# A two-layer decoder trunk on one core: norm factors applied to projection results, and the first layer's gate units moved ahead of its attention

## The chip, the cores and the metric

One core of a Trainium2 chip runs one launch of the whole step. The metric is device time in microseconds (us) of that launch. The median of three runs of the kernel before is 1759.73 us (1757.77 to 1759.96).

## What is computed

The tokens are 512 of a prompt and 64 of eight samples (8 each), 576 columns in all, with a model width of 1024. Two layers follow each other:

```
for layer in (0, 1):
    h = rms_norm(x, g_mix[layer])
    # layer 0: forgetting attention (8 heads of 64) || spatial gating of width 512
    # layer 1: stick-breaking attention            || short gated convolution of width 512
    x = x + concat(attention(h), side(h)) @ w_out
    h = rms_norm(x, g_mlp[layer])
    x = x + square(relu(h @ w_up)) @ w_down        # 1024 -> 4096 -> 1024
y = rms_norm(x, g_final)

rms_norm(x, g) = x * rsqrt(mean(x*x) + 1e-6) * g    # one factor per token, one gain per channel
```

The samples attend to 1024 past positions each, gathered page by page (128 rows) from caches in HBM: 64 pages of keys and 64 of values per layer, 256 KB each. Besides y, the new keys, values, log forget gates, normalised gate rows and convolution tails are outputs.

Two facts matter below. The factor of a token (call it r) is the same for all channels, so it can be multiplied in before a projection or into its result. And the gain g depends on the channel, so it has to be in the input.

## The kernel before, in words

**Layout.** Activations lie with channels on the 128 partitions and the 576 tokens along the free dimension: X (the residual stream) is 8 chunks of 128x576. Products are taken in a split form: every operand is cut into a high part and a low rest (HH and HL for activations, WH and WL for weights), and a product is the sum of high x high, low x high and high x low.

**Units.** All projections are done in units. A unit is one 128-column block of weights (WR, 128x1024, 512 KB) against all 576 tokens: 8 chunks x 3 products x 2 halves of 288 tokens = 48 matmuls into a pair of PSUM banks (`unit`, L1395; the body loop of `unit_loop`, L209). There are 188 units: 4 + 12 + 4 in the first layer's input projection (4 gate columns "g", 12 for q, k and v, 4 for the side branch), 8 for its output, 64 for its MLP, and 24 + 8 + 64 in the second layer. ScalarE cuts the high part of the weights two units ahead (`cut_high`, `next_high`, L531 to L547), VectorE takes the rest (`cut_low`, L846), and SyncE loads the raw block once the rest is cut (`load_weights`, L362). There are two sets of weight buffers and two pairs of banks for units. Semaphores count: `unit_done` (TensorE), `evac_act` and `evac_dve` (a result has left PSUM), `w_high`, `w_low`. A unit starts when its weights are cut and both engines have emptied the unit two before it.

**Norm** (`norm`, L583 and L890; `rms`, L1418; `pair_after_norm`, L1415). After the last unit of a stage, ScalarE squares the chunk, VectorE adds it to SQS, TensorE multiplies SQS by ones to sum over channels, VectorE and ScalarE turn that into R (the factor r, laid out on all partitions), and then for each of 8 chunks VectorE multiplies X by gain and R into TMP, ScalarE cuts HH, VectorE takes HL. The first two units of the next stage are interleaved chunk by chunk (`first_pair`), so that they can follow the chunks.

**Attention** (20 slots, `for k in range(SLOTS)`, L1683 on TensorE, L761 on ScalarE, L1295 on VectorE). A slot handles one of 16 prompt tasks (a pair of heads and a block of 128 queries) in four steps spread over slots, four key pages (`page`: 4 turns of 128x128 into PSUM bank BK, then one copy to KTB by ScalarE or VectorE) and a share of the samples' work. The side branch's units are cut in halves (`half_unit`, L1663, 24 matmuls into bank BU) and laid between: the first layer's 8 halves one each in slots 0 to 7, the second layer's 24 in slots 0 to 17. The next page's turns wait until the last page has been copied, since both use BK:

```
if n >= 1:
    name, count = page_copied(L, n - 1)
    pe.wait_ge(S[name], count)
```

**Queues.** SyncE issues all large loads in program order and waits in that order. GpSimd issues 64 small loads of the cached log gates (`lf_raw`, L478), the constants of the gating branch and the stores. The first layer's order on TensorE is: turn x, norm 0, the four g units, wait for all `lf_raw`, forget logits, turn g, twelve q/k/v units with the gating products between them, turn k and v to rows, attention.

**End.** After the last unit: norm 4 writes Y, TensorE turns Y, VectorE copies it to XN (L1375), and GpSimd issues two stores (L520, L521).

## Time and profile before

| | us |
|---|---|
| median of three runs | 1759.73 |
| the profiled execution | 1760.2 |
| its span in the trace | 1758.2 |
| TensorE matmul busy | 1560.7 (89%) |
| TensorE weight load busy | 1446.0 (82%) |
| VectorE busy | 737.9 (42%) |
| ScalarE busy | 527.2 (30%) |
| GpSimd busy | 54.0 (3%) |

The span is what the trace covers from the first instruction to the last; the execution's own time has about 2 us around it. Matmuls are pipelined, so a busy TensorE says that matmuls were in flight, not that the array is at its peak: what a unit costs is read from how long a run of units takes. Busy shares are averages over stages with different limits, and so the views by stage count more than this table. The granted TensorE clock averages 0.942 of full speed over the span.

### The profile page before, as it was taken

How to read it: one execution, taken by the hardware profiler on the slowest of the kernel's cores; microseconds unless marked ns; L12 is line 12 of the kernel's file. 1: busy time of each engine (PE TensorE's matmuls, PEld its weight loads, DVE VectorE, ACT ScalarE, POOL GpSimd, SP SyncE). 2: the span in 40 equal slices, each digit the busy share in tenths (PEclk: the TensorE clock that was granted, in tenths of full speed). 3: DMA queues.
4: the chain of work that ended last, by engine and by line, in shares of the span. 5: the costliest groups of instructions: out<-in, count | busy, mean ns of one | idle time of the engine just before them, and what ended most of it. 6: DMA issues, size and time to landing. Idle time of an engine off the chain costs nothing.

```text
span 1758.2 us, 31539 instructions
## 1 busy us (share of the span) xinstructions
PE 1560.7 (89%) x12022; PEld 1446.0 (82%) x12022; DVE 737.9 (42%) x1142; ACT 527.2 (30%) x860; POOL 54.0 (3%) x124
## 2 busy tenths in 40 slices
PE   4599988777889999999989998887789999999994
PEld 3599865446889999999989886665689999999994
DVE  5244444432444434343352355556354433434334
ACT  3121233321233313132232245556133322313120
POOL 4410000000000000000000000000000000000000
PEclk9799899887989999999989999999889999999997
DMA  4123356642212223323242345664222222222221
GB/s 141 40 80 86 121 150 198 189 142 84 84 48 84 84 76 87 87 73 94 73 132 84 108 141 155 194 181 138 65 72 60 84 85 83 85 83 84 84 72 54
DMA packets 239074, 178.65 MB, mean 102 GB/s; under 512 B 9860, under 2 KB 203464, under 8 KB 238986
## 3 DMA queue, kind: packets, MB, share of 16 engines
q1 hardware_dynamic: 234282, 168.62, 33.2%
q0 software_dynamic: 4704, 8.88, 1.5%
q8 instruction: 53, 0.87, 0.2%
q14 instruction: 35, 0.29, 0.1%
HBM read 170.20 MB, written 7.26 MB: 101 GB/s over the span
## 4 chain that ended last, share of the span: by engine, by line
PE 81%; DVE 5%; ACT 5%; issue 4%; DMA 2%; POOLq 1%; POOL 1%; SPq 1%; DVEq 0%; ACTq 0%
PE BP L1395 58%; PE BU L1673 4%; PE BP L1410 4%; PE BK L1547 4%; PE BD L1656 2%; PE BD L1628 2%; PE BP L1585 1%; POOLq L477 1%; PE BK L1608 1%; PE BP L1598 1%; ACT WH L537 1%; ACT KTB L654 1%; PE BD L1635 1%; DVE WL L848 1%; POOL lf_raw L478 1%
## 5 line engine op out<-in xcount | busy, mean ns | idle before, releaser
L1395 PE MATMUL BP<-HH,WH 128*128 128x288 f32 x1536 | 332.8, 299 | 18.4 <-DVE ffL L886 7.9
L1395 PE MATMUL BP<-HL,WH 128*128 128x288 f32 x1536 | 331.2, 298 | 0.0
L1395 PE MATMUL BP<-HH,WL 128*128 128x288 f32 x1536 | 331.0, 298 | 0.0
L848 DVE TENSOR_TENSOR WL<-WR,WH 128x1024 fp32r<-128x1024 f32 x188 | 230.1, 1224 | 105.2 <-ACT WH L537 73.1
L1395 PEld LDWEIGHTS BP<-HH,WH 128*128 128x128 f32 x1536 | 250.4, 191 | 19.7 <-ACT TMP L576 8.3
L1395 PEld LDWEIGHTS BP<-HL,WH 128*128 128x128 f32 x1536 | 250.4, 191 | 0.0
L1395 PEld LDWEIGHTS BP<-HH,WL 128*128 128x128 f32 x1536 | 250.0, 191 | 0.0
L547 ACT ACTIVATE WH<-WR 128x1024 fp32r<-128x1024 f32 x159 | 167.2, 1051 | 240.8 <-PE BP L1395 240.4
L1395 PE MATMUL BP<-ffH,WH 128*128 128x288 f32 x1024 | 218.9, 295 | 0.0
L1395 PE MATMUL BP<-ffL,WH 128*128 128x288 f32 x1024 | 218.3, 294 | 0.0
L1395 PE MATMUL BP<-ffH,WL 128*128 128x288 f32 x1024 | 216.9, 293 | 0.0
L872 DVE TENSOR_TENSOR X<-BP,X 128x288 f32 (+1 forms) x160 | 65.8, 453 | 263.8 <-PE BP L1395 263.8
L1395 PEld LDWEIGHTS BP<-ffL,WH 128*128 128x128 f32 x1024 | 163.7, 188 | 0.0
L1395 PEld LDWEIGHTS BP<-ffH,WL 128*128 128x128 f32 x1024 | 163.7, 187 | 0.0
L1395 PEld LDWEIGHTS BP<-ffH,WH 128*128 128x128 f32 x1024 | 162.9, 187 | 0.0
L884 DVE TENSOR_TENSOR TMP<-TMP 128x576 f32<-128x576 f32 x64 | 48.5, 758 | 168.8 <-ACT TMP L576 168.8
L1547 PEld LDWEIGHTS BK<-ident,KR 128*128 128x128 f32 x512 | 61.2, 150 | 65.1 <-issue 59.4
L1547 PE MATMUL BK<-ident,KR 128*128 128x128 f32 x512 | 87.4, 297 | 27.1 <-ACT KTB L654 16.9
L576 ACT ACTIVATE TMP<-BP 128x288 f32<-128x288 f32 x128 | 45.5, 408 | 199.6 <-PE BP L1395 199.6
L654 ACT ACTIVATE KTB<-BK 128x512 f32<-128x512 f32 x80 | 47.7, 596 | 148.5 <-PE BK L1547 143.6
L1138 DVE COPY KTB<-BK 128x512 f32<-128x512 f32 x48 | 33.2, 691 | 124.8 <-PE BK L1547 121.8
L1673 PE MATMUL BU<-HH,WH 128*128 128x288 f32 x256 | 79.4, 310 | 0.0
(296 smaller groups left out, 1738.1 us busy)
## 6 DMA issues: line engine op xcount, KB each, us to landing
WR<-in_w_up_dram SPq DMA_DIRECT2D x64, 512.0 KB, 4.1
WR<-in_w_down_dram SPq DMA_DIRECT2D x64, 512.0 KB, 3.9
KR<-in_cache_fox_k_dram SPq DMA_DIRECT2D x64, 256.0 KB, 2.8
VR<-in_cache_fox_v_dram SPq DMA_DIRECT2D x64, 256.0 KB, 3.0
VR<-in_cache_sb_v_dram SPq DMA_DIRECT2D x64, 256.0 KB, 3.2
KR<-in_cache_sb_k_dram SPq DMA_DIRECT2D x64, 256.0 KB, 2.8
WR<-in_w_in_odd_dram SPq DMA_DIRECT2D x24, 512.0 KB, 4.1
WR<-in_w_in_even_dram SPq DMA_DIRECT2D x20, 512.0 KB, 4.0
```

The source lines that it names most:

```text
L547: A(WH[1 - u][:], WR[1 - u][:], ACT.Copy).then_inc(S["w_high"], 1)
L576: last = A(TMP[:, u, h * TH:(h + 1) * TH], B[2 * u + h][:, 0:TH], ACT.Relu)
L654: A(KTB[:, n // 4 % 2, :, n % 4 * P:(n % 4 + 1) * P], BK[:, :].rearrange("p (c k) -> p c k", c=CT), ACT.Copy).then_inc(S["kt_act"], 1)
L848: V.tensor_tensor(WL[u][:], WR[u][:], WH[u][:].bitcast(F32), ALU.subtract).then_inc(S["w_low"], 1)
L872: last = V.tensor_tensor(x, B[2 * u + h][:, 0:TH], x, ALU.add)
L884: V.tensor_tensor(TMP[:, u, :], TMP[:, u, :], TMP[:, u, :], ALU.mult).then_inc(S["relu_squared"], 1)
L1395: last = M(B[2 * u + h][:, 0:TH], w[u][:, k, :], x[:, k, h * TH:(h + 1) * TH], start=(k == 0 and n == 0), stop=(k == KT - 1 and n == 2))
L1410: last = M(B[2 * u + h][:, 0:TH], w[u][:, k, :], x[:, k, h * TH:(h + 1) * TH], start=(m == 0 and n == 0), stop=(m == KT - 1 and n == 2))
L1547: last = TR(BK[:, c * P:(c + 1) * P], KR[:, n % 4, c * P:(c + 1) * P], ident[:])
L1628: last = M(BD[32 * c:32 * c + 32, o * 512:(o + 1) * 512], QB[:, c, p, s:s + 2, :], KTB[:, grp % 2, c, :], start=(L == 1 and s == 0), stop= ...
L1656: last = M(B5[32 * c:32 * c + 32, 0:P], PTS[:, 4 * (g % 2) + jj, c, s:s + 2, :], v_tile(g, jj)[:, c * P:(c + 1) * P], start=False, stop=(g ...
L1673: last = M(BU[:, 0:TH], w[u][:, k, :], x[:, k, h * TH:(h + 1) * TH], start=(k == 0 and n == 0), stop=(k == KT - 1 and n == 2))
```

## The change

It has these parts.

1. **The factor r leaves the input.** The high and low parts of an activation chunk are now cut from X times gain alone (`lift` on ScalarE, `lift_low` on VectorE), right after that chunk's residual unit has been added (`evac_lift`). r (tile R, or R1 for the second layer's input projection) is multiplied in as VectorE empties a unit's banks (`evac_in`, `evac_up`), since VectorE now empties both halves. `evac_act` is gone. The first unit of a stage waits chunk by chunk for `norm_low`, and the sum of squares and its matmuls come behind that unit.
2. **A third weight set** for unit 2 of each output projection and of the first stage, with banks 4 and 5; its cutting waits for no unit.
3. **The start.** x is loaded in two column halves with the first two weight blocks between them; turns of x and chunks of the first pair alternate; the constants of the gating branch are loaded early by SyncE.
4. **The first layer's order.** Forget logits and the cached log gates come after ten of the twelve q/k/v units. The four side units are whole units before the attention, with the turns of k and v among them. Turns of g, k and v use two banks. No half units are left in the first layer's attention.
5. **First layer's attention.** Key pages alternate between banks BK and BU (`page_bank`); the samples' `sample_top` and `sample_exp` come one slot earlier.
6. **The second layer's side branch** takes three multiplications of a 128x576 tile by R1 for each of four blocks, on GpSimd, and VectorE's `conv_in` and `gate_half` wait for them (`side_scaled`).
7. **The MLP** reads its input from new tiles H2H and H2L; HH and HL serve as one of the two buffers of the hidden layer. relu and r are one VectorE operation out of PSUM; the square moves to ScalarE.
8. **The end.** Y is X times gain; its turns lie between the last units (`turn_y`), r is found per row with a small matmul, and rows are scaled and stored one block of 128 rows after the other by SyncE.

Of the diff, its core, in the order of the file: planning, then SyncE, GpSimd, ScalarE, VectorE and TensorE.

```diff
+        def page_bank(L, n):
+            return B[6 + n % 2] if L == 0 else B[6]
...
-        SIDE_OUT = [{9: (0, 1), 10: (2, 3)}, {18: (0, 1, 2, 3)}]
+        SIDE_OUT = [{1: (0, 1), 2: (2, 3)}, {18: (0, 1, 2, 3)}]
...
+            load_x(0)
...
+            load_first(0)
+            load_first(1)
+            load_x(1)
+            load_first(2)
...
                 if L == 1:
+                    for c in range(CT):
+                        for step2 in range(3):
...
+                            g.tensor_tensor(RES[:, c, :], RES[:, c, :], R1[:], ALU.mult).then_inc(S["side_scaled"], 1)
...
+            def lift(z):
+
+                dst = {1: H2H, 2: HH, 3: H2H, 4: Y}[z]
                 def body(g, i, u, more):
                     next_high(g, u, more)
...
+                    act.wait_ge(S["evac_dve"], g + 3)
+                    gain = vec[:, NORM_G[z] + i:NORM_G[z] + i + 1]
+                    if z < 4 or i < KT - 1:
+                        A(dst[:, i, :], X[:, i, :], ACT.Copy, scale=gain).then_inc(S["norm_high"], 1)
+                    A(TMP[:, u, :], X[:, i, :], ACT.Square).then_inc(S["squared"], 1)
...
-                        last = A(TMP[:, u, h * TH:(h + 1) * TH], B[2 * u + h][:, 0:TH], ACT.Relu)
-                    last.then_inc(S["evac_act"], 1)
...
+                    act.wait_ge(S["up_relu"], i + (m0 + 1))
+                    A(TMP[:, u, :], TMP[:, u, :], ACT.Square).then_inc(S["relu_squared"], 1)
...
+            def evac_in(tile_of, r, scale=None):
...
                     for h in range(2):
...
+                        if scale is None:
+                            last = V.tensor_tensor(t, z, s, ALU.mult)
+                        else:
+                            last = V.scalar_tensor_tensor(t, z, scale, s, ALU.mult, ALU.mult)
                     last.then_inc(S["evac_dve"], 1)
...
+            def lift_low(z, k, dst, src):
+
+                gain = vec[:, NORM_G[z] + k:NORM_G[z] + k + 1]
+                dve.wait_ge(S["norm_high"], z * KT + k + 1)
+                V.scalar_tensor_tensor(dst[1][:, k, :], X[:, k, :], gain, dst[0][:, k, :].bitcast(F32), ALU.mult, ALU.subtract
+                                       ).then_inc(S["norm_low"], 1)
...
+                    for h in range(2):
+                        s = slice(h * TH, (h + 1) * TH)
+                        last = V.scalar_tensor_tensor(TMP[:, u, s], B[2 * u + h][:, 0:TH], 0.0, R[:, s], ALU.max, ALU.mult)
+                    last.then_inc(S["up_relu"], 1)
                     dve.wait_ge(S["ff_high"], i + (m0 + 1))
...
+            def unit(hi, lo, z=None):
+                def body(g, i, u, more=None, mid=None, wset=None, bank=None):
                     pe.wait_ge(S["w_low"], g + 3)
-                    pe.wait_ge(S["evac_act"], g + 1)
-                    pe.wait_ge(S["evac_dve"], g + 1)
...
                     for k in range(KT):
+                        if z is not None:
+                            pe.wait_ge(S["norm_low"], z * KT + k + 1)
...
+                    unit_loop(pe, unit(HH, HL), q + 8, 2)
+                    past_rows()
+                    forget_logits()
+                    unit_loop(pe, unit(HH, HL), q + 10, 2)
+                    forget_turn()
+                    past_tail()
+                    pe.wait_ge(S["evac_dve"], q + 12 + 2)
+                    natural(NG, 2 * NG, 2)
+                    unit_loop(pe, unit(HH, HL), G_SIDE[0], 2)
+                    forget_sums()
+                    natural(2 * NG, 3 * NG, 2)
+                    unit_loop(pe, unit(HH, HL), G_SIDE[0] + 2, 2)
...
-                    if n >= 1:
-                        name, count = page_copied(L, n - 1)
+                    back = 2 if L == 0 else 1
+                    if n >= back:
+                        name, count = page_copied(L, n - back)
                         pe.wait_ge(S[name], count)
...
+                        if n == 0:
+                            first = 2
+                            unit(H2H, H2L, 1 + 2 * L)(g, 0, 0)
+                            rms(1 + 2 * L)
+                            unit(H2H, H2L)(g + 1, 1, 1)
```

Three places show the new order. The first is TensorE at the start of the program, before the change; XN holds x as rows, BP are the banks of the units.

```order
L1434 MATMUL BP<-ident,XN 128x128 x4
L1435 MATMUL BP<-ident,XN 128x64
L1421 MATMUL BP<-SQS,ones 128x288 x2
L1410 MATMUL BP<-HH,WH_55 128x288 x2
L1410 MATMUL BP<-HL,WH_55 128x288 x2
L1410 MATMUL BP<-HH,WL_57 128x288 x2
```

And after it:

```order
L1587 MATMUL BD<-ident_62,XN_91 128x128 x4
L1588 MATMUL BD<-ident_62,XN_91 128x64
L1556 MATMUL BP0<-HH_50,WH0_55 128x288 x2
L1556 MATMUL BP0<-HL_51,WH0_55 128x288 x2
L1556 MATMUL BP0<-HH_50,WL0_57 128x288 x2
L1556 MATMUL BP1<-HH_50,WH1_56 128x288 x2
L1556 MATMUL BP1<-HL_51,WH1_56 128x288 x2
L1556 MATMUL BP1<-HH_50,WL1_58 128x288 x2
L1587 MATMUL BK<-ident_62,XN_91 128x128 x4
```

The sum of squares no longer stands between the turns of x and the first unit; a turn and a chunk of the first pair alternate.

The second is VectorE between the last unit of the first output projection and the first units of the MLP, before the change; WL_57 and WL_58 are the two low weight sets.

```order
L876 TENSOR_TENSOR SQS<-SQS,TMP 128x576
L220 REGISTER_ALU
L220 COMPARE_AND_BRANCH
L848 TENSOR_TENSOR WL_58<-WR_54,WH_56 128x1024
L894 TENSOR_SCALAR R<-BP 128x288 x2
L896 MEMSET SQS 128x576
L902 SCALAR_TENSOR_TENSOR TMP<-X,vec,R 128x576 x2
L911 TENSOR_TENSOR HL<-TMP,HH 128x576
```

And after it:

```order
L949 TENSOR_TENSOR X<-BP,X 128x288 x2
L960 SCALAR_TENSOR_TENSOR H2L<-X,vec,H2H 128x576
L965 TENSOR_TENSOR SQS<-SQS,TMP 128x576
L922 TENSOR_TENSOR WL_58<-WR_54,WH_56 128x1024
L1005 TENSOR_SCALAR R<-BD 128x288 x2
L1007 MEMSET SQS 128x576
L993 SCALAR_TENSOR_TENSOR TMP<-BP,R 128x288 x2
L996 TENSOR_TENSOR HL<-TMP,HH 128x576
L922 TENSOR_TENSOR WL_57<-WR_53,WH_55 128x1024
```

The chunk's low part (H2L) is cut before R exists; R now stands ahead of the first result's way out of PSUM, and the next weight block (WL_57) behind it.

The third is TensorE in slots 1 and 2 of the first layer's attention, before the change; L1547 are turns of a key page, L1673 a half unit, L1628 the samples' scores.

```order
L1547 MATMUL BK<-ident_62,KR_92 128x128 x12
L1585 MATMUL BP0<-PA_90 128x128 x2
L1589 MATMUL BP0<-FR_110,twin_71 128x128 x2
L1591 MATMUL BP0<-neg_causal_r_69,ident_r_64 128x128 x2
L1626 MATMUL BD<-DR_109,PICK_128 128x512
L1628 MATMUL BD<-KTB_104,QB_127 32x512 x4
L1547 MATMUL BK<-ident_62,KR_92 128x128 x4
L1673 MATMUL BU<-HH_50,WH1_56 128x288
L1673 MATMUL BU<-HL_51,WH1_56 128x288
L1673 MATMUL BU<-HH_50,WL1_58 128x288
```

And after it:

```order
L1722 MATMUL BK<-ident_62,KR_94 128x128 x4
L1722 MATMUL BU<-ident_62,KR_94 128x128 x4
L1760 MATMUL BP0<-PA_92 128x128 x2
L1764 MATMUL BP0<-FR_115,twin_71 128x128 x2
L1766 MATMUL BP0<-neg_causal_r_69,ident_r_64 128x128 x2
L1801 MATMUL BD<-DR_114,PICK_136 128x512
L1803 MATMUL BD<-KTB_109,QB_135 32x512 x4
L1722 MATMUL BK<-ident_62,KR_94 128x128 x4
L1722 MATMUL BU<-ident_62,KR_94 128x128 x4
L1803 MATMUL BD<-KTB_109,QB_135 32x512 x4
```

The half unit has gone from between the pages, and the pages alternate between two banks.

## Rows read from the trace of the kernel before

**Rows 1.** The page: TensorE's busy time, and its granted clock in 40 slices.
```profile
PE 1560.7 (89%) x12022; PEld 1446.0 (82%) x12022; DVE 737.9 (42%) x1142; ACT 527.2 (30%) x860; POOL 54.0 (3%) x124
...
PEclk9799899887989999999989999999889999999997
```

**Rows 2.** Stretches: length, busy us by engine (instructions), granted clock, DMA share, GB/s.
```profile
101.67:197.20 95.53, 95.53 (x731) 93.00 (x729) 40.91 (x76) 19.74 (x31) 6.53 (x13) 1.00 0.28 76
197.20:291.30 94.10, 79.64 (x691) 61.63 (x689) 39.77 (x96) 25.64 (x58) 2.32 (x4) 0.91 0.59 180
291.30:381.30 90.00, 70.10 (x627) 43.83 (x626) 36.99 (x80) 29.52 (x74) 0.00 (x0) 0.87 0.62 182
381.30:416.66 35.36, 20.96 (x214) 12.77 (x213) 12.28 (x26) 9.05 (x21) 0.00 (x0) 0.74 0.43 126
416.66:475.60 58.94, 55.53 (x384) 55.07 (x384) 20.10 (x29) 11.55 (x14) 0.00 (x0) 0.93 0.23 66
475.60:503.84 28.24, 16.90 (x100) 16.16 (x101) 18.86 (x27) 11.40 (x18) 0.00 (x0) 0.82 0.13 36
503.84:899.40 395.56, 395.53 (x2976) 395.29 (x2976) 153.54 (x193) 109.02 (x160) 0.00 (x0) 1.00 0.29 82
899.40:925.61 26.21, 17.01 (x105) 16.25 (x105) 17.81 (x26) 11.07 (x16) 0.52 (x1) 0.80 0.56 162
992.00:1242.82 250.82, 209.04 (x1901) 163.30 (x1901) 134.49 (x220) 129.87 (x219) 4.23 (x7) 0.92 0.54 159
1301.70:1329.91 28.21, 16.85 (x101) 16.11 (x101) 18.87 (x27) 11.41 (x18) 0.00 (x0) 0.82 0.13 36
1725.50:1758.20 32.70, 9.83 (x44) 7.24 (x44) 15.61 (x30) 2.05 (x3) 1.30 (x2) 0.61 0.20 72
```

**Rows 3.** TensorE in order of time, the start: us, length, idle before it and its releaser.
```profile
11.86 1.11 PE L1434 MATMUL BP<-ident,XN 128*128 128x128 f32 x4
...
38.23 0.82 PE L1410 MATMUL BP<-HH,WH 128*128 128x288 f32 x2 [4.88 <-DVE HL L911]
...
86.78 0.48 PE L1460 MATMUL BU<-ident,lf_raw 64*128 64x64 f32 x2 [16.73 <-DMA lf_raw<-in_cache_fox_logf_dram]
```

**Rows 4.** TensorE's waits in the first layer's attention (197 to 416 us): total, times, longest.
```profile
PE BK L1547 <- ACT KTB L654: 13.8, 16, 2.1
PE BD L1635 <- ACT SN L731: 10.1, 4, 3.9
```

**Rows 5.** The half units alone (L1673), first eight slots and next eight: us, busy, clock.
```profile
197.20:291.30 94.10, 27.99 (x192) 26.34 (x192) 0.91 0.59 180
```

**Rows 6.** Two page turns, in order of time, and a stretch of slots without half units.
```profile
338.40 0.65 PE L1547 MATMUL BK<-ident,KR 128*128 128x128 f32 x4
...
362.15 1.12 PE L1547 MATMUL BK<-ident,KR 128*128 128x128 f32 x4
...
319.50:350.20 30.70, 23.59 (x234) 14.56 (x234) 15.87 (x34) 13.16 (x35) 0.00 (x0) 1.00 0.71 206
```

**Rows 7.** TensorE at unit 2 of the first output projection, in order of time.
```profile
435.34 0.70 PE L1395 MATMUL BP<-HH,WH 128*128 128x288 f32 x2 [3.31 <-ACT TMP L563]
```

**Rows 8.** Groups of instructions: busy us, mean ns of one | idle before, releaser.
```profile
L848 DVE TENSOR_TENSOR WL<-WR,WH 128x1024 fp32r<-128x1024 f32 x188 | 230.1, 1224 | 105.2 <-ACT WH L537 73.1 <-ACT WH L547 24.9
L547 ACT ACTIVATE WH<-WR 128x1024 fp32r<-128x1024 f32 x159 | 167.2, 1051 | 240.8 <-PE BP L1395 240.4 <-issue 0.2
L872 DVE TENSOR_TENSOR X<-BP,X 128x288 f32 x148 | 60.9, 453 | 257.4 <-PE BP L1395 257.4
L884 DVE TENSOR_TENSOR TMP<-TMP 128x576 f32<-128x576 f32 x64 | 48.5, 758 | 168.8 <-ACT TMP L576 168.8
L579 ACT ACTIVATE ffH<-TMP 128x576 f32 x60 | 41.1, 686 | 55.4 <-DVE TMP L884 55.4
L460 POOL TENSOR_SCALAR_AFFINE_SELECT upto<-upto 128x128 f32<-128x128 f32 x1 | 0.3, 282 | 0.0
```

801 lines of the change are left out of this document (465 added, 336 removed).

## The prediction, made before the changed kernel had run

> **What bounds the kernel now.** I read the page first, then the trace by stretches, then the waits inside the stretches where TensorE stands still. In the page TensorE's matmuls are in flight for 89% of the span and the granted clock is at its upper level (2.4 GHz, a 9 in the row of slices) except near the stage ends and in the attentions [rows 1]. The stretches say what kind of bound that is. In the first MLP 62 units take 395.56 us, 6.38 us each or 0.133 us per matmul, with TensorE busy all the time at clock 1.00 [rows 2]: there only fewer matmuls would help, and the change removes none. But each stage end is a hole: 28.24, 26.21 and 28.21 us for one norm and a first pair, in which 96 of the 100 to 105 matmuls are the pair's, at a clock of 0.80 to 0.82 [rows 2]. The last 32.70 us hold 44 matmuls [rows 2]. In the first layer's attention TensorE is busy 79.64 of 94.10 and 70.10 of 90.00 us [rows 2]. So what this change can gain lies in the holes, and I price each hole by what of it has to stay. The sum stands against the profiled execution of 1760.2 us, 0.5 above the median of the three runs; I subtract from the median.
>
> **1. Start to attention (0 to 197.2 us).** Gone from the path: the sum of squares and the factor before the first unit (which started at 38.23 [rows 3]) and the 16.73 us for the 64 small gate loads [rows 3], now waited for ten units later. The first pair may start once half of x and two weight blocks are there and cut: turns began at 11.86 [rows 3], and a cut is 1.05 + 1.22 us [rows 8], so between 12 and 16, and I take 13. Then 96 matmuls x 0.133 = 12.8, six turns laid between (4 + 1 instructions, 0.85 us at full clock from 0.65 [rows 6]) = 5.1, and 3.5 more since the early part will run at the lower clock (a turn took 1.11 us [rows 3]): 34.4. Two more gate units (12.8) and the moved sum of squares (0.9) end at 48.1, or about 48.7 with hand-offs, where they ended at 70.05 (86.78 less its idle time, [rows 3]): -21.3. The loads' wait goes with about 2 us of lower clock behind it: -18.7. The four side units come in: 4 x 6.38 = +25.5. SyncE gets eleven small loads of gating constants ahead of unit 3's block, which TensorE wants some 28 us later than the first: free. Against that stand new joints: k and v are turned in two banks instead of four, so that each turn waits for the copy two before it, forget logits and log-gate rows stand between units with VectorE's new evacuations ahead of them, and the attention begins behind an evacuation and not behind a turn. No row shows them; bounds are 2 us (all covered) and 22 us (every one of 15 turns waits 0.8 and a few long waits); I take 12, since such a single-bank wait costs about 0.86 us each (13.8 in 16 [rows 4]). Together **-2.5**, ends -12 and +8.
>
> **2. First layer's attention (197.20 to 416.66, 219.5 us).** Eight half units leave: 27.99 us of matmuls [rows 5]. What that is worth is open. The slots with halves took 94.10 us, the next eight without 90.00 [rows 2]: a difference of 4.1, the lower bound; 28.0 is the upper. Slots 8 to 15 do more of the samples' work and ran at 0.87 instead of 0.91, so 4.1 is too little; and a half covered copies and transfers. I take -18. The waits for a key page's copy, 13.8 us in 16 [rows 4], are what two banks remove, with some 2.5 us of shorter ones: -16.3. `sample_exp` one slot earlier answers the four waits for SN, 10.1 us [rows 4]; I leave 2: -8. The first output weights are now loaded and cut inside the attention, where the rest of the block (1.22 us [rows 8]) and its hand-offs used to hold the first output pair: -3.2. Sum -45.5, taken as **-46**, ends -26 and -75. What comes next as a bound is the transfers: 128 pages of 256 KB are 33.6 MB, and at the 206 GB/s seen without halves [rows 6] that is 163 us, just under the 173.5 that I forecast; the far end would need 232 GB/s.
>
> The clock is the doubt here. A page turn took 0.65 us at the upper level and 1.12 at the lower (1.2 GHz) [rows 6]; but 319.50:350.20, a stretch without any half unit, had clock 1.00 throughout, with 234 matmuls busy 23.59 of 30.70 us [rows 6]. From that row I count no further loss. The Trainium skill, "TensorE: Matmul & The Clock Gate", Part 4, says that transposes in PE mode don't count as activity for the full clock; by that rule, taking the half units from between the turns would leave the array idle in the clock's eyes. The trace disagrees for the stretch named, since it is mostly turns and scores; by the rule term 2 would be about +27 instead of -46, and the total 1730 (rival A).
>
> **3. Output projections.** Unit 2 waited 3.31 us for banks and weights [rows 7], and so did the second layer's; the third set and banks 4 and 5 remove both, and about 1.2 us of lower clock behind each: **-9**, ends -6 and -11.
>
> **4. The three norm transitions.** The pair's 96 matmuls at 0.133 are 12.8 us, and the sum's two matmuls about 1.24; the rest of 28.24, 26.21 and 28.21 [rows 2] is 14.2, 12.2 and 14.2. It goes if the first unit of the next stage follows the last residual unit. It can: after each residual unit VectorE does two additions of 453 ns, one low cut (about 0.76) and a sum of squares (0.76), a weight rest (1.22), together 3.7 us; ScalarE copy, square and high cut, about 2.5 us [rows 8]; both below 6.38. Only the last chunk is late: 0.9 + 0.69 + 0.76 is 2.4 us behind its unit, while the first unit's seven earlier chunks last 5.6 us. What comes late next is R: first needed when unit 0 leaves PSUM, it is ready about 2.4 us after the sum; with two relu operations, square, copy and a low cut (0.9 + 0.69 + 0.69 + 0.76, and 1.22 for a weight rest in between) the chain is about 7.2 us against unit 1's 6.38. So about 1 us comes back twice, at each MLP's start: -40.6 + 2.6 = **-38**, ends -30 and -42.
>
> **5. The end.** Of the 32.70 us [rows 2], the norm, turns and copies after the last unit shrink to: last addition 0.9, last chunk's Y and square 1.4, sum and factor about 3, scaling and store of a block of 512 KB. I keep 19.9. The turns of Y now lie between units: 7 x 0.75 = +5.3 on a busy TensorE. **-7.5**, ends -12 and -4.
>
> **6. Second layer's attention (250.82 us).** TensorE is busy 209.04 of it, VectorE 134.49 [rows 2]. GpSimd gets 12 multiplications of 128x576. The one near row is 282 ns for 128x128 [rows 8]; by elements that is 1.27 us each, 15.2 in all, on an engine with 4.23 us of work in this stretch [rows 2]. The side branch's results are needed only at the last slot. **0**, ends 0 and +15 (all of it held against VectorE, or the last block late). If the cover by half units were gone, each of the four blocks would cost its 3.8 us.
>
> **7. The MLP units.** VectorE takes over ScalarE's relu out of PSUM and ScalarE the square. Per up unit VectorE: 2 x 0.45, 0.76 and 1.22 = 2.9 us; ScalarE: 0.69 + 0.69 + 1.05 = 2.4 us; both below 6.38. 0, end +2.
>
> Sum: -2.5 - 46 - 9 - 38 - 7.5 = -103. **1759.7 - 103 = 1657 us.**
>
> **Rivals.**
> A, the clock falls in the first layer's attention. With no long units between the pages the stretch stays at the lower level. For it: the clock is 0.74 in 381.30:416.66, where the least work is dense [rows 2]; page turns then cost 1.12 for 0.65 [rows 6]. Against it: the row of 1.00 without halves [rows 6]. Price: TensorE's work there is 79.64 + 70.10 + 20.96 - 27.99 = 143 us [rows 2, 5]; times 1.12 / 0.65 it is 246, with no wait left, where I forecast 173: +73, 1730. A partial fall, +20 to +40, is likelier than the full one.
> B, GpSimd holds VectorE. The twelve multiplications stand in the side branch's chain and run beside VectorE's work on the same tiles. Price +15: 1672. The Trainium skill, "GPSIMD Engine Reference", sections 3.1 and 4.1, gives an elementwise operation of two inputs on GpSimd about twice VectorE's time (4497 against 2293 ns for 2048 elements) and says that the two share SBUF ports; an estimate from that is 1.26 us for 576 elements. No row of this kernel shows the sharing.
> C, the transitions don't close. If the first unit still waits for the stage's end (its low chunk held by the weight rest ahead of it on VectorE, or the sum of squares ahead of the cut), term 4 is about -5: 1690. Against it: in the order of the changed kernel the low cut stands directly behind the additions.
> D, slower than before, in the up-projections. The chain from a unit's end to the next use of its buffers is now two VectorE operations, square, copy, low cut and the two weight cuts on the same engines: 0.9 + 0.69 + 0.69 + 0.76 + 1.05 + 1.22 = 5.3 us with everything in a row. It decides once it exceeds 6.38; it would have to be 8.0 us (2.7 us of hand-offs) for 64 up units to lose 103 us and end above 1760. For it: VectorE now does what two engines did at every unit's exit, and TensorE's next unit waits on that alone. Against: busy sums of 2.9 and 2.4 us.
>
> **How the numbers follow.** The forecast, with its terms inside their ends, has 0.72; A in full 0.04, in part 0.09; B 0.07; C 0.05; D 0.03, mostly past the point where it ends above 1760. The independent ends added as squares give about -20 and +35 around 1657, so the forecast's own range is 1637 to 1692; a part of A, and a gain beyond my ends in the attention, are to be held too: **1630 to 1700**. Outside lie A in full, most of D and a little on either side of the forecast, together under 0.2. A measurement here tells about 0.2%, 3.5 us, from no change; only D and a full A with B and C reach it: faster 0.96, same 0.01, slower 0.03.
>
> **What would show it.** In the changed profile: the first matmul of the first pair (L1556) at 13 us and q units from 48; the attention from about 195, with key turns alternating BK and BU and few waits for KTB, no wait of 3.9 us for SN, ending near 368 at a mean clock of at least 0.87; no idle time over 4 us on TensorE at the three stage ends, but about 1 us at the MLPs' third unit; up and down units at 6.38 us; the second attention within 2 us of 250.8; a tail near 20 us. It is wrong if the granted clock of the first attention is under 0.75 (A), if TensorE waits for `side` work or conv steps in the second (B), if the first unit's idle time names norm_low of an early chunk (C), or if units of the MLP take more than 6.5 us (D).

## The result, and the profile after

The changed kernel takes 1626.75 us (median of 4, 1626.14 to 1632.39); the kernel before, run beside it, 1758.75 (1756.65 to 1759.96). The ratio is 0.9258 with a 95% interval of 0.9235 to 0.9281: faster by 132 us, where 103 were forecast. The time lies 3 us below the stated range of 1630 to 1700.

The page of the changed kernel, the rows that answer to [rows 1]:

```profile
PE 1520.4 (94%) x12030; PEld 1412.5 (87%) x12030; DVE 730.4 (45%) x1200; ACT 518.5 (32%) x776; POOL 65.2 (4%) x123
...
PEclk9999999989999999999999999898899999999998
```

TensorE runs 12030 matmuls where it ran 12022: the work is nearly the same, and what has gone is time in which it stood or ran slowly. The mean granted clock went from 0.942 to 0.970.

The stretches that answer to [rows 2]: start; first attention; first output projection; transition to the MLP; the other 62 units of the first MLP; second norm and input projection; second attention; output projection; transition; second MLP with the turns of Y; the tail. Columns as there.

```profile
0.00:191.23 191.23, 173.02 (x1244) 164.23 (x1245) 95.59 (x197) 43.08 (x55) 41.19 (x102) 0.99 0.41 112
191.23:355.37 164.14, 134.61 (x1332) 85.67 (x1333) 74.69 (x158) 57.30 (x147) 0.52 (x1) 0.90 0.66 196
355.37:407.70 52.33, 52.33 (x386) 52.33 (x387) 26.59 (x40) 16.55 (x22) 0.00 (x0) 0.98 0.22 64
407.70:421.43 13.73, 13.73 (x101) 13.29 (x99) 7.25 (x12) 6.00 (x8) 0.00 (x0) 1.00 0.25 73
421.43:815.30 393.87, 393.29 (x2979) 393.29 (x2979) 161.27 (x232) 113.66 (x138) 0.00 (x0) 1.00 0.29 86
815.30:894.36 79.06, 78.14 (x586) 77.50 (x584) 28.41 (x45) 15.39 (x16) 0.51 (x1) 1.00 0.36 104
894.36:1146.64 252.28, 209.81 (x1900) 161.53 (x1901) 138.04 (x221) 130.81 (x220) 22.95 (x19) 0.91 0.53 158
1146.64:1199.20 52.56, 52.56 (x385) 52.56 (x386) 24.96 (x36) 15.16 (x20) 0.00 (x0) 0.97 0.25 72
1199.20:1213.01 13.81, 13.81 (x102) 13.36 (x100) 7.25 (x12) 6.00 (x8) 0.00 (x0) 1.00 0.25 73
1213.01:1610.20 397.19, 396.61 (x3008) 396.61 (x3009) 158.87 (x234) 112.60 (x137) 0.00 (x0) 1.00 0.27 80
1610.20:1624.50 14.30, 2.49 (x20) 2.13 (x18) 7.53 (x16) 1.94 (x6) 0.00 (x0) 0.63 0.44 165
```

Read it as a ledger. The transitions are now pure matmul time: 13.73 us busy of 13.73, where [rows 2] shows 16.90 of 28.24. The second norm with the input projection, which after the change is the stretch 815.30:894.36, was before it

```profile
899.40:992.00 92.60, 82.76 (x585) 81.79 (x586) 34.92 (x48) 24.13 (x35) 0.52 (x1) 0.93 0.36 103
```

so that the whole ledger, forecast beside measured, is this (profiled executions; each measured number is the difference of unrounded lengths above and in [rows 2]; before the change the second output projection was 1242.82:1301.70 and the second transition with its MLP 1301.70:1725.50):

| stage | before | after | measured | forecast |
|---|---|---|---|---|
| start | 197.2 | 191.2 | -6.0 | -2.5 |
| first attention | 219.5 | 164.1 | -55.3 | -46 |
| output projections | 58.9 + 58.9 | 52.3 + 52.6 | -12.9 | -9 |
| three transitions with what follows | 423.8 + 92.6 + 423.8 | 407.6 + 79.1 + 407.7 | -45.9 | -38 |
| second attention | 250.8 | 252.3 | +1.5 | 0 |
| tail, with Y's turns between units | 32.7 | 14.3 + 3.3 | -15.1 | -7.5 |
| sum | 1758.2 | 1624.5 | -133.7 | -103 |

(The 3.3 is 397.19 less 393.87: seven turns of Y, 0.47 us each; it is taken out of the second MLP's 411.0 and put to the tail.) The signs are right (for the second attention nothing was forecast), and every gain was put too low: the miss of 30 us is spread over the stages, with 9.3 in the first attention, 7.9 in the transitions, 7.6 in the tail, 3.9 in the output projections and 3.5 in the start.

What TensorE still waits for between 190 and 400 us (total, times, longest):

```profile
PE BD L1818 <- ACT PTS L815: 6.5, 4, 1.6
PE BD L1831 <- DMA VR<-in_cache_fox_v_dram: 6.4, 5, 3.1
PE BD L1827 <- DVE PTN L1400: 5.3, 4, 1.6
...
PE BK L1722 <- ACT KTB L717: 1.2, 2, 0.8
```

KTB's 13.8 us in 16 waits [rows 4] are down to 1.2 in 2, and SN's 10.1 in 4 to 0.3 in 1. The waits for the samples' next steps and for the value pages' transfers grew a little: PTS was 3.5 before the change, PTN 4.0, VR 5.1.

### The profile page after: what moved, and what is told of

Its sections match the earlier page's. It is cut to its first block, busy times and chain, and to the rows that moved or that the text cites. A ratio compares the mean times of both kernels' runs of the same rounds, so it can differ in the third digit from the quotient of the medians.

```text
span 1624.5 us, 30903 instructions
## 1 busy us (share of the span) xinstructions
PE 1520.4 (94%) x12030; PEld 1412.5 (87%) x12030; DVE 730.4 (45%) x1200; ACT 518.5 (32%) x776; POOL 65.2 (4%) x123
## 4 chain that ended last, share of the span: by engine, by line
PE 85%; DVE 5%; ACT 4%; issue 2%; SPq 2%; DMA 2%; POOL 0%; DVEq 0%; ACTq 0%
PE BP L1547 64%; PE BU L1848 3%; PE BP L1556 3%; PE BK L1722 2%; PE BD L1831 2%; PE BD L1803 2%; PE BD L1547 1%; PE BP L1760 1%; SPq L436 1%; DMA VR<-in_cache_fox_v_dram 1%; ACT PP L724 1%; SPq L437 1%; PE BP L1773 1%; ACT KTB L717 1%; PE BD L1638 0%
## 5 line engine op out<-in xcount | busy, mean ns | idle before, releaser
L1547 PE MATMUL BP<-HH,WH 128*128 128x288 f32 x1120 | 239.8, 296 | 0.5 <-DVE WL L922 0.5
L1547 PE MATMUL BP<-HH,WL 128*128 128x288 f32 x1120 | 238.8, 295 | 0.0
L1547 PE MATMUL BP<-HL,WH 128*128 128x288 f32 x1120 | 238.7, 295 | 0.0
L1547 PE MATMUL BP<-H2H,WH 128*128 128x288 f32 x1024 | 218.8, 295 | 1.2 <-DVE WL L922 1.2
L1547 PE MATMUL BP<-H2L,WH 128*128 128x288 f32 x1024 | 218.8, 294 | 0.0
L1547 PE MATMUL BP<-H2H,WL 128*128 128x288 f32 x1024 | 217.2, 293 | 0.0
L1547 PEld LDWEIGHTS BP<-HH,WH 128*128 128x128 f32 x1120 | 179.7, 188 | 1.1 <-DVE WL L922 0.7
L1547 PEld LDWEIGHTS BP<-HH,WL 128*128 128x128 f32 x1120 | 179.8, 188 | 0.0
L1547 PEld LDWEIGHTS BP<-HL,WH 128*128 128x128 f32 x1120 | 179.8, 188 | 0.0
L1547 PEld LDWEIGHTS BP<-H2H,WH 128*128 128x128 f32 x1024 | 163.2, 187 | 1.8 <-issue 1.6
L1547 PEld LDWEIGHTS BP<-H2H,WL 128*128 128x128 f32 x1024 | 163.8, 188 | 0.0
L1547 PEld LDWEIGHTS BP<-H2L,WH 128*128 128x128 f32 x1024 | 163.4, 188 | 0.0
L1547 PE MATMUL BP<-ffL,WH 128*128 128x288 f32 x512 | 109.5, 294 | 0.0
L1547 PE MATMUL BP<-ffH,WH 128*128 128x288 f32 x512 | 109.4, 295 | 0.0
L1547 PE MATMUL BP<-ffH,WL 128*128 128x288 f32 x512 | 108.7, 293 | 0.0
L993 DVE SCALAR_TENSOR_TENSOR TMP<-BP,R 128x288 f32<-128x288 f32 x128 | 52.6, 452 | 118.6 <-PE BP L1547 116.9
```

Of the source, the lines that this page charges most:

```text
L993: last = V.scalar_tensor_tensor(TMP[:, u, s], B[2 * u + h][:, 0:TH], 0.0, R[:, s], ALU.max, ALU.mult)
L1547: last = M(B[b + h][:, 0:TH], w[w0][:, k, :], x[:, k, h * TH:(h + 1) * TH], start=(k == 0 and n == 0), stop=(k == KT - 1 and n == 2))
```

## The experiments

A word on noise first. The first layer's attention, from the first key-page turn to the first output pair, is the same code in eleven of the kernels profiled here (the changed one among them), and took 164.1 to 169.7 us in them, mean 166; the second layer's, from its first key-page turn, 244 to 253.5 in all. So a difference of totals of 5 us, or of 9 where single profiles are compared, says little, and I read an edit's effect in its own stretch of the trace. Differences of the first attention are given against the changed kernel's 164.1; against the mean they are 2 us smaller.

### The first layer's attention

**One bank for key pages.** In the changed kernel:

```diff
-            return B[6 + n % 2] if L == 0 else B[6]
+            return B[6]
...
-                    back = 2 if L == 0 else 1
+                    back = 1
```

> The changed kernel with one bank for the first layer's key pages again. My theory, by the prediction's term 2: the second bank is worth the 13.8 us of KTB waits and 2.5 us of shorter ones, so this kernel takes 14 to 18 us more than 1626.75. Rival: since the half units are gone and the pages now follow each other directly, a single bank would show a wait on nearly every one of 64 pages; at 0.8 us each that is up to 50 us. Second rival: the attention is bound by its loads, and one bank costs under 5 us.

Measured 1660.17 us (+33), and the attention took 193.4 instead of 164.1: +29.3. The waits and the first slots:

```profile
PE BK L1722 <- ACT KTB L717: 21.8, 23, 2.0
```
```profile
192.50:275.00 82.50, 65.58 (x492) 41.66 (x493) 29.68 (x59) 23.79 (x58) 0.52 (x1) 0.73 0.44 128
```

With 2.5 us more for VectorE's copies the waits for KTB come to 24.3, against 2.1 in the changed kernel: 22 us more, of which other waits give back some 4. The other part of the 29 is clock: it is 0.73 here, while the changed kernel's first stretch of this attention shows 0.95 (below), and the same 1332 matmuls are in flight for 146.45 us instead of 134.61, 11.8 more. The forecast of 16.3 was off by the factor 1.8.

**Short half units.** In the kernel before, each first-layer half unit has 2 matmuls instead of 24:

```diff
-                    for k in range(KT):
+                    ks = (0, KT - 1) if L == 0 else range(KT)
+                    for k in ks:
                         for n, (w, x) in enumerate(((WH, HH), (WH, HL), (WL, HH))):
+                            if L == 0 and n != (0 if k == 0 else 2):
+                                continue
```

> The kernel before, with each of the first layer's eight half units cut from 24 matmuls to 2 (the side branch's gate results are left out, their handling stays). It takes off 25.7 of the 28.0 us of matmuls and nothing else. By the prediction's term 2 the path gains 18: 1741 against 1759. Rival one: page copies and clock eat it, gain 4 or less. Rival two (clock, rival A of the prediction): with the long stretches of matmuls gone the granted clock of 197 to 291 us falls clearly under 0.91 and the kernel gains nothing or loses. Rival three: the whole 25.7 shows.

Measured 1747.93 (ratio 0.9923, 0.9901 to 0.9945), 10.6 us less than before; the attention took 211.5 instead of 219.5. So 25.7 us of matmuls were worth 8 (one profile of each kernel; like stretches of the changed kernel differ by up to 5.6). Why, its first slots show:

```profile
198.80:290.00 91.20, 68.50 (x534) 44.17 (x531) 40.94 (x98) 25.82 (x59) 2.26 (x4) 0.79 0.63 195
```
```profile
PE BK L1547 <- ACT KTB L654: 13.7, 13, 5.9
```

The clock fell from 0.91 [rows 2] to 0.79, and in this stretch the KTB waits rose to 13.7 us from this, in the kernel before:

```profile
PE BK L1547 <- ACT KTB L654: 6.0, 6, 2.1
```

This is rival A's mechanism, in part: half units had filled the waits and held the clock up.

**Filler with one bank** tests that the other way round. The kernel with one bank gets work of the half units' size in slots 0 to 7:

```diff
+                    if L == 0 and k < 2 * CT:
+                        pe.wait_ge(S["w_low"], G_OUT[0] + 4)
+                        for n in range(27):
+                            j2 = 2 * (n % 4)
+                            M(BU[:, 0:2 * P], (WH[0] if n % 2 else WL[0])[:, n % KT, :], WH[1][:, j2:j2 + 2, :].rearrange("p k n -> p (k n)"),
+                              start=(n == 0), stop=(n == 26))
```

> The changed kernel with one bank for key pages, and in each of the first layer's slots 0 to 7, where a half unit stood before the change, 27 matmuls of 256 columns on weights that lie there (results not used): about 25 us of TensorE work. The kernel with one bank takes 193.4 us in the attention. If such work covers the waits for page copies and holds the clock up, as the 8.0 us for 25.7 us of matmuls in the kernel with short half units suggests, the attention takes about 202. Rival: work and waits add, and it takes 218.

Measured 202.6 us in the attention, 1666.83 in all. Some 25 us of extra work (216 matmuls, in flight 29.31 us) cost 9.2. The first slots:

```profile
190.70:285.00 94.30, 82.24 (x744) 62.91 (x748) 32.44 (x65) 25.74 (x64) 0.52 (x1) 0.95 0.45 130
```

The clock is 0.95 where it was 0.73, and the KTB waits are 14.2 us where they were 21.8. The covering is seen from both sides: taking such work out gives 8, putting it in costs 9.

**Samples' exp a slot later**, as before the change:

```diff
+                        if p >= 0 and o == 1:
+                            sample_top(p)
...
-                        if p >= 0 and o == 0:
-                            sample_top(p)
```

(and the same for `sample_exp`).

> The changed kernel with the samples' sample_top and sample_exp of the first layer back one slot later, where they were before. By term 2: four waits of TensorE for SN of 2.0 to 2.5 us come back, +8, and perhaps more by lower clock behind them. Rival: the weights are needed no sooner than the second half of their slot, and under 2 us come back.

Measured 1641.48 (+15); the attention 175.2, +11.1, with TensorE's waits for SN at 13.0 us in 4 where the changed kernel has 0.3. As forecast in kind, 3 more in size.

**Late cut of the second output block:**

```diff
-                    cut_high(G_OUT[0] + 1)
...
-                if L == 1:
-                    cut_high(G_OUT[1] + 1)
+                cut_high(G_OUT[L] + 1)
```

(and `cut_low` likewise).

> The changed kernel with the cut of the second output weight block at the end of the first layer's attention again. By term 2 the wait before the first output pair comes back: +3.2; the second layer, where this wait is still there, shows 4.55 us, so +4.5 in the attention's stretch, up to +6 with lower clock. Rival: the pair starts behind the last values' transfers anyway: under 1.

```profile
PE BP L1552 <- DVE WL L920: 3.2, 1, 3.2
```

Measured 1634.04 (+7). The wait is back with the 3.2 us that term 2 had for it; the attention took 170.0, which is hardly outside the noise.

**Those three undone together.**

> The changed kernel with three parts of the first layer's attention undone together: one bank for key pages, sample_top and sample_exp a slot later, and the cut of the second output weight block at the attention's end. If the parts add up as measured alone (29.3 and 11.1 us in the attention's stretch) and the cut is worth 3.3 to 4.5, the stretch takes 164.1 + 29.3 + 11.1 + 4 = 208, close to the 211.5 of the kernel before with short half units. Rival: the parts overlap (waits of one cover those of the other, the clock falls only once), and it takes under 200.

Measured 209.3 us in the attention (sum forecast 208), 1669.39 in all. The parts add up, and what is left to the 211.5 us of the kernel before with short half units is 2.2. Its clock over the whole attention, against that of one bank and of the filler:

```profile
192.20:401.50 209.30, 155.86 (x1332) 96.63 (x1332) 76.22 (x163) 60.85 (x149) 0.52 (x1) 0.80 0.51 152
```
```profile
192.50:385.90 193.40, 146.45 (x1332) 92.23 (x1333) 74.24 (x158) 58.71 (x147) 0.52 (x1) 0.85 0.56 166
```
```profile
190.70:393.30 202.60, 162.54 (x1548) 114.08 (x1549) 74.26 (x158) 58.95 (x147) 0.52 (x1) 0.92 0.55 160
```

The same 1332 matmuls are busy for 134.61 us at clock 0.90 in the changed kernel, 146.45 at 0.85 and 155.86 at 0.80: a hole costs its own length and then the slower matmuls near it.

### The transitions and output projections

**All chunks first.** The first unit waits for all eight low chunks:

```diff
-                            pe.wait_ge(S["norm_low"], z * KT + k + 1)
+                            pe.wait_ge(S["norm_low"], z * KT + KT)
```

> The changed kernel, but the first unit of each of the three stages waits for all eight low chunks before its first matmul instead of for each in turn. The last chunk is ready about 2.4 us after its residual unit: +2.4 x 3 = 7, and up to 1.7 us of lower clock behind each hole: +7 to +12. Rival: since all but the last chunk are ready long before, and the clock doesn't fall for so short a hole: +6 or less.

Measured 1641.96 (+15); in the trace three waits like this one (the last addition, high cut and low cut of term 4, 2.4 there):

```profile
PE BP L1547 <- DVE H2L L960: 2.7, 1, 2.7
```

That is 8.0 us of idle time, and behind one of the three the clock fell as well (1.7 us); from the first output pair on, without the second attention, the kernel is 10.1 us longer. The rest of the 15 lies in the start (1.8), the first attention (0.6) and the second (250.5 against 247.9, 2.6), which is noise.

**Sum first.** The sum of squares' matmuls ahead of the first unit:

```diff
-                            unit(H2H, H2L, 1 + 2 * L)(g, 0, 0)
                             rms(1 + 2 * L)
+                            unit(H2H, H2L, 1 + 2 * L)(g, 0, 0)
```

> The changed kernel with the sum of squares' matmuls ahead of the first unit in the three norm transitions, so that TensorE stands until the last chunk has been squared and added. By my theory only this order and the chunkwise start close the transitions: last addition 0.9, low cut 0.8, square 0.7, addition 0.8 gives 3 to 4 us of idle each and up to 1.7 us of lower clock behind it: +9 to +15 in all, R is then ready earlier, which gives back 0.6 twice. Rival: the transitions close because r has left the input, and the place of the sum matters little: under 5 us.

Measured 1643.52 (+17); three waits of this kind:

```profile
PE BD L1572 <- DVE SQS L965: 3.2, 1, 3.2
```

By the same reckoning this kernel is 11.7 us longer: 9.7 of idle time, and a dip of the clock behind two of the three holes (0.67 and 0.63 in the next 4 us), none behind the first (1.00).

Neither order brings back the 14 us of each old transition. The other 11 us of each I put to what stood before the first matmul only because r was in the input (mean, root, the multiplication by r, the cuts behind it); no run puts r back there, so this cause is argued and not shown.

**Two weight sets.** Unit 2 of both output projections on the ordinary set and banks:

```diff
-            return 2 if g == 2 else 3 if g - 2 in (G_OUT0, G_OUT1) else 0
+            return 2 if g == 2 else 0
```

(and its loads, cuts and banks as for any unit).

> The changed kernel with unit 2 of both output projections on the ordinary weight set and banks again. By term 3 the waits of 3.3 us come back, and 1.2 to 1.7 us of lower clock behind each: +9. Rival: the first pair's two evacuations are now short and early, so only the cuts (1.05 + 1.22) stand after it: +2.3 x 2, under 6.

Measured 1640.69 (1633.86 to 1644.03); in the output stretches two waits of 2.7 us, and the stretches from the first pair to the next sum of squares grew from 58.6 and 58.9 to 61.4 and 63.7: +7.6. The second grew more since the clock was at 0.57 for 3.94 us behind its hole, and at 1.00 behind the first. Between the two readings (6 and 9).

### The MLP units: where VectorE would decide

In each up unit VectorE's relu is done three times (the extra results go into tiles that are overwritten later), and in a second kernel the extra ones in pieces of 72 columns:

```diff
+                    for again in (ffL, ffH):
+                        for n in range(2):
+                            s = slice(n * 288, (n + 1) * 288)
+                            V.scalar_tensor_tensor(again[grp % 2][:, ds(i, 1), s].rearrange("p o t -> p (o t)"), B[2 * u + n // 1][:, n % 1 * 288:(n % 1 + 1) * 288], 0.0, R[:, s], ALU.max, ALU.mult)
```

> The changed kernel with VectorE's relu out of PSUM done three times over in each of 64 up units (two extra results overwritten later): +1.8 us of VectorE per unit, in the chain in front of the square. By the prediction's rival D the chain of 5.3 us would become 7.1 against 6.34 for a unit: +0.76 x 64 = +49. By the other reading VectorE has 2.9 + 1.8 = 4.7 us of work per unit, the chain has two units to end in, and nothing changes: within 2 us.

> As the kernel with the relu done three times, but the two extra results in 16 pieces of 128x72, which should add about 3.6 us of VectorE per up unit: 6.5 us of work against 6.34 for a unit. By the chain reading (rival D) +2.5 x 64 = +160. By the reading that VectorE's sum of work decides, +0.2 x 64 = +13 (0 to +40, as the pieces' duration is not known).

Measured 1641.67 (+15) and 1671.03 (+44); 13.7 and 41.3 us of it in the two MLPs. The chain is seen on VectorE in the changed kernel, one up unit and the next (start, length):

```profile
435.01 0.82 DVE L993 SCALAR_TENSOR_TENSOR TMP<-BP,R 128x288 f32<-128x288 f32 x2 [1.77 <-PE BP L1547]
437.52 0.76 DVE L996 TENSOR_TENSOR HL<-TMP,HH 128x576 f32 x1 [1.69 <-ACT HH L637]
438.39 1.22 DVE L922 TENSOR_TENSOR WL<-WR,WH 128x1024 fp32r<-128x1024 f32 x1
441.36 0.82 DVE L993 SCALAR_TENSOR_TENSOR TMP<-BP,R 128x288 f32<-128x288 f32 x2 [1.74 <-PE BP L1547]
```

and in the kernel with pieces:

```profile
435.08 1.21 DVE L994 SCALAR_TENSOR_TENSOR HL<-BP,R 128x72 f32 x8 [0.29 <-PE BP L1551]
436.21 1.20 DVE L994 SCALAR_TENSOR_TENSOR HH<-BP,R 128x72 f32 x8
437.33 0.81 DVE L997 SCALAR_TENSOR_TENSOR TMP<-BP,R 128x288 f32<-128x288 f32 x2
439.72 0.76 DVE L1000 TENSOR_TENSOR HL<-TMP,HH 128x576 f32 x1 [1.57 <-ACT HH L637]
440.67 1.23 DVE L922 TENSOR_TENSOR WL<-WR,WH 128x1024 fp32r<-128x1024 f32 x1 [0.19 <-ACT WH L603]
```
```profile
PE BP L1551 <- DVE WL L922: 21.3, 46, 2.8
```

A unit's low weights are ready 4.6 us after the unit ahead ended (435.01 to 439.61) in the changed kernel, and 6.8 us (435.08 to 441.90) in the one with pieces; a unit lasts 6.34. So 0.5 us per up unit is over, and 44 / 64 = 0.69 was measured. With three whole relus it is just at the edge (4.6 + 1.8 = 6.4): almost no hole in the matmuls, but the weight loads between units begin to wait (PEld busy 49.26 of 50 us in 430 to 480 us, 50.00 in the changed kernel), and the wait at the MLP's start grows from 0.6 to 2.0. The pieces added 2.2 us and not the 3.6 I expected, and the chain was 4.6 and not 5.3, so the +49 and +160 that I had by rival D's chain were far too much. **The chain reading is still the right one**: VectorE is busy only 36.24 of the 50 us from 430 to 480 in the kernel with pieces, and its own work in such a unit is 5.2 us (1.21 + 1.20 + 0.81 + 0.76 + 1.23), under 6.34, so that the sum of work would have cost nothing. But in the changed kernel the chain has 1.7 us of room, so rival D lost on its number.

### GpSimd in the second attention

The twelve multiplications cut to two columns each:

```diff
-                            g.tensor_tensor(RES[:, c, :], RES[:, c, :], R1[:], ALU.mult)
+                            g.tensor_tensor(RES[:, c, 0:2], RES[:, c, 0:2], R1[:, 0:2], ALU.mult)
```

> The changed kernel with GpSimd's twelve multiplications of the second layer's side branch cut to two columns each (the factor is left out of the rest). By term 6 they are hidden: within 2 us. By rival B they hold VectorE or the side branch: 5 to 15 us less.

Measured 1629.83 (1627.28 to 1632.30), no less than the changed kernel; the second attention took 246.9 us against 247.9. Rival B's 5 to 15 us aren't there. In the changed kernel the group is

```profile
L569 POOL TENSOR_TENSOR RES<-RES,R 128x576 f32<-128x576 f32 x12 | 18.7, 1558 | 169.1 <-ACT RES L770 93.1 <-DVE RES L1353 75.6
```

1558 ns each, longer than the 1.27 us of term 6, and hidden.

### The start and the end

**Both halves of x first**, ahead of the first two weight blocks.

> The changed kernel with both halves of x loaded ahead of the first two weight blocks. The second half is 1 MB and a part; in the changed kernel x's first half was turned from 8.6 us and the pair began at 16.5, held by the cut of the weights. With the second half ahead, the weights land about 4 us later, and so does the pair: +4. Rival: the copies and cuts of chunks bound the start, not the landing: within 1 us.

Measured 1633.30 (+6.6), of which 4.0 in the start; the second attention, at 253.5 the longest of all, makes up the rest. The first matmul of the pair, in the changed kernel and then here:

```profile
16.48 0.82 PE L1556 MATMUL BP<-HH,WH 128*128 128x288 f32 x2 [3.77 <-DVE WL L922]
```
```profile
20.03 0.82 PE L1556 MATMUL BP<-HH,WH 128*128 128x288 f32 x2 [3.77 <-DVE WL L922]
```

3.6 us later, as expected.

**The gates' wait early**, after four units:

```diff
+                    pe.wait_ge(S["lfp_in"], 16 * NB * PG)
                     unit_loop(pe, unit(HH, HL), q, 2)
```

> The changed kernel in which TensorE waits for the 64 small loads of the cached gates after four units, as before the change, without anything else moved. They landed at 86.8 us in the kernel before; the four units now end at 48.8. If they land as late as before, TensorE stands 38 us: +38 and 2 of lower clock. If they land earlier now, since the queues are laid otherwise, the difference is the landing less 48.8.

```profile
PE BP L1547 <- DMA lf_raw<-in_cache_fox_logf_dram: 34.9, 1, 34.9
```

Measured 1663.62 (+37): the loads land at 84 us now, hardly earlier than before. Had the wait stayed in its place, the four units' gain of 21 us would have come down to 3 (83.8 against 86.8); where it stands now, TensorE finds them landed.

**Turns of Y last.** All eight turns and copies behind the last unit.

> The changed kernel with all eight turns of Y and their copies after the last unit, as before the change, but r still found per row and the stores still by block. The measured tail fell by 18.5 us and 7 turns of 0.5 us came between units. If the turns' place is what the tail gained by, this kernel takes about 7 copies x 0.9 + the turns at the lower clock, less 3.5, so +4 to +8. Rival: the tail is short because the norm is a row factor and the stores go out by block; then it is within 3 us.

**Stores last.** All stores of y after the last scaling.

> The changed kernel with the stores of y issued only after the last block has been scaled, instead of each block after its own scaling. Four scalings of 0.7 us are what the first store gains: +2.5 to +4, all of it in the tail of 14.4 us. Rival: the last block's store ends the kernel either way, since the stores before it run beside the scalings: within 1 us.

Measured 1635.94 and 1633.87. Their tails, 20.3 and 16.8 us against 14.3:

```profile
1614.90:1635.20 20.30, 7.67 (x50) 6.19 (x48) 11.86 (x26) 1.94 (x6) 0.00 (x0) 0.70 0.32 117
```
```profile
1614.80:1631.60 16.80, 2.35 (x21) 2.00 (x19) 7.53 (x16) 1.94 (x6) 0.00 (x0) 0.65 0.38 140
```

Turns between units buy 6.0 and cost 3.3 on TensorE: 2.7 net. Storing by block buys 2.5. (The totals rose by more, 9.2 and 7.1; both kernels' first attentions, the same code, were 5.6 and 3.1 us longer.) Of the 18.4 us by which the tail fell, 8.5 are these two if they add, and the other 9.9 I put to r as a factor of a row: in the trace before, mean and root of 576 columns and the multiplications for Y stand ahead of the turns, and now they don't. No run separates that part, so it is argued and not shown.

### A version that beats both

Two waits left in the changed kernel are at the attentions' ends: the last value pages (up to 3.1 and 4.1 us), and 4.6 us for the second output block of the second layer. Of the edits that go at them, the core:

```diff
+                    if s == NGRP + 1:
+                        sp.wait_ge(S["k_turned"], NB * PG * (L + 1))
+                        for jj in range(4):
+                            q = v_page(L, NPAIR - 1, 3, jj)
+                            v = sp.value_load(pages[0:1, q:q + 1], min_val=0, max_val=POOL - 1)
+                            sp.dma_start(KR[:, jj, :], cache_v[L][0][ds(v, 1)].rearrange("o p h d -> (o p) (h d)")
+                                         ).then_inc(S[f"k_in{L}_{jj}"], 16)
...
+                        if k == NTASK + 2:
+                            cut_high(G_OUT[1] + 1)
```

> The first of these two edits alone. My theory: the waits for the last value pages go, 4 to 9 us less than the changed kernel. Rival: the loads are only moved against others, within 2 us.

> The changed kernel with two further edits: the last four value pages of each layer go to the key pages' buffers, free by then, and are loaded two slots earlier; and the second output block of the second layer is cut in slot 18 instead of behind the attention. The waits in question are 1.6 + 3.1 us in the first layer, 1.2 + 4.1 in the second, and 4.55 at the second pair: 14.6 in all. If nothing else takes their place: 8 to 14 us under the changed kernel, about 1615. Rival: the values' transfers are bound by the queue and the 4.55 hides behind the attention's results: under 4.

Measured 1622.64 (1622.37 to 1625.18) and 1619.49 (1618.26 to 1622.02); the latter's ratio to the kernel before is 0.9214 (0.9193 to 0.9234). Together -7 against the changed kernel, half of the 14.6 us of waits. What is left or new at the second attention's end:

```profile
PE BD L1848 <- DVE RD L1415: 3.2, 2, 2.8
PE BP L1562 <- issue: 2.1, 1, 2.1
```

The first line stood in the changed kernel too (3.3 us in 2); the second is new, in place of the 4.6 for the weights. The waits for value pages at the two ends fell from 4.7 and 5.3 us to 1.1 and 1.5. The profiles bear out less than the totals: they differ by 5.9 us, 2.0 and 2.2 of it in the two attentions. And of the first edit alone the profile shows nothing in the attentions (164.1 and 247.4 us against 164.1 and 247.9), and the interval of its ratio (0.9212 to 0.9248) overlaps the changed kernel's, so that a gain by it isn't shown; the interval of both edits lies just below.

## Why the prediction was wrong

The direction held, and where a run undoes a part, its mechanism did too; the sum was 30 us short, and the steps that failed are the sizes of terms 2, 4, 5, 3 and 1, in the order of their misses, and the range put together from the terms' ends.

**Term 2, the first attention (-46, measured -55.3).** "What two banks remove, with some 2.5 us of shorter ones: -16.3" failed. I priced the second bank by the waits of the kernel before [rows 4], but these waits were what was left after half units had covered others; the same change takes the half units away. One bank without them costs 29.3. For the same reason "I take -18" for the half units was too much: 8.0. Each error had the other's sign, and the sum of the two was near (34.3 against 37.3), since it is the pair that counts. The rest is `sample_exp` at 11.1 (my 8 left 2 us of wait that didn't stay), and the early cut at 3.2 as forecast. The sum of the parts, 29.3 + 11.1 + 3.2 + 8.0 = 51.6, leaves 4 of the 55.3 within the noise of this stretch.

**Rival A** was half true: with half units gone and nothing else changed, the clock did fall (0.91 to 0.79). It didn't in the changed kernel, because the second bank took the holes away at the same time. Its first 70 us, turns and scores without a single unit:

```profile
191.23:261.50 70.27, 60.95 (x568) 39.61 (x569) 37.86 (x74) 28.07 (x71) 0.52 (x1) 0.95 0.64 191
```

is at 0.95; with one bank the like stretch is at 0.73, with the same kinds of matmuls. The rule of the Trainium skill in "TensorE: Matmul & The Clock Gate", Part 4, that turns in PE mode don't count as activity, is neither borne out nor refuted here: turns are some 27 of the 60.95 us in flight, and the rest, for scores, values and sums, may have held the clock up. In the row without half units that I set against the rule [rows 6] it is the same: 10 of 23.59 us are turns, so "mostly turns and scores" was too much. What the runs do show is that one and the same set of matmuls ran at mean clocks from 0.90 down to 0.80, by the waits between them.

**Term 4, the transitions (-38, measured -45.9)** failed at "about 1 us comes back twice" (its sum had 2.6 for both): 0.6 came back twice. The larger part is that I had left out the clock behind a hole: the first units of the old MLP ran like this,

```profile
503.84:507.20 3.36, 3.36 (x14) 3.36 (x15) 2.42 (x3) 1.64 (x2) 0.00 (x0) 0.50 0.38 114
```

3.36 us at the lower of the two levels, outside the stretch of 28.24 us that I priced. That is 1.7 us of lost time for this transition, and it went with the hole. The other two lost as much (0.75 and 0.85 in 925.61:928.50 and 928.50:935.00, 0.51 in 1329.91:1333.30), so that 5.1 of the 7.9 us missed are the clock. It also made my 6.38 us per unit too long (395.56 less 1.7, over 62, is 6.35; after the change 6.34).

**Term 5, the tail (-7.5, measured -15.1)** failed at "I keep 19.9": 14.3 stayed, and the turns cost 3.3 instead of 5.3. The turns between units cost 0.47 us each and not 0.75: their matmuls start 0.11 us after one another, and the next unit's right behind. The other part, 5.6 us, is the shorter tail, for which I had named steps but no row.

**Term 3 (-9, measured -12.9)** failed at "about 1.2 us of lower clock behind each" and at the pairs' start. Behind the two holes the clock was 0.53 for 3.60 us (435.40:439.00) and 0.51 for 3.50 us (1261.50:1265.00), 1.7 us each. And the pairs themselves began at the lower level in both kernels, but left it earlier after the change: 0.50 in 416.66:420.00 and 0.76 in the next 4 us before, 0.55 in 355.37:358.00 and then 1.00 after, 1.4 us in the first layer and 1.0 in the second. With the waits of 3.3 that makes 12.4. Of this, undoing the third set alone gave 7.6.

**Term 1 (-2.5, measured -6.0):** the four units ended at 48.8, as forecast (48.7), but by luck: the pair began at 16.5, not 13, and the 3.5 us put down for a lower clock weren't there (the clock was 1.00 in 16.48:48.85). What failed is "I take 12" for the joints: they come to 8.5 us, few waits among them, 1.7 us for RES, 0.8 for WFL and under 1 each for the copies of turned rows.

**Terms 6 and 7** held: the second attention is within its noise, up and down units are at 6.34. Rivals B and C are refuted by the multiplications' run and by transitions without a hole, D by its margin. (That GpSimd and VectorE share SBUF ports, which rival B took from the Trainium skill, stands on that page in section 1, "Specifications", and not in 3.1 or 4.1.)

The range failed with them, for two reasons. Its arithmetic was wrong: the terms' own ends below the forecast are 9.5, 29, 2, 4 and 4.5 us, and added as squares they give 31 and not "about -20" (above it 29 and not 35). That would have put the low end at 1626, and the measured 1626.75 just inside, almost by the width of the attention's end alone. And terms 3, 4 and 5 lie beyond their own ends (-11, -42, -12): I had rounded each unknown joint towards cost (12 for the start, 2 left of SN, 19.9 of the tail), and such choices add instead of cancelling.

## What to carry to other kernels

Don't price the removal of a wait by the wait's present length if the same change takes away work that covered it: price the pair, by the slots where the cover is absent. Look behind every hole of TensorE for slower matmuls, outside the stretch in which the hole lies: here they cost 1.7 us behind some holes of 2.7 to 4 us, and nothing behind others of the same length. And when all unknowns are rounded to the careful side, say so and move the range's low end down by their sum.

## What the runs showed that I had not expected

- Extra work can be cheap in a stretch with holes: 25 us of matmuls cost 9.2 there, since the granted clock rose from 0.73 to 0.95 and the waits shrank by 7.6 us.
- The same 1332 matmuls of the first attention are in flight 134.6, 146.5 or 155.9 us, in stretches of 164.1, 193.4 and 209.3 us at granted clocks of 0.90, 0.85 and 0.80.
- The second attention, the same code in most kernels, varied by 9.5 us between profiles (244.0 to 253.5), more than the four runs of the whole changed kernel (1626.14 to 1632.39).
- A 128x576 multiplication of two tiles on GpSimd took 1558 ns. The Trainium skill, "GPSIMD Engine Reference", section 3.1, led to an estimate of 1.26 us; the measurement decides.
